# Seven row buffers, x1 parked in DRAM, h2 in one run and a shorter expert search in a fused transformer layer

## What is computed

```
h2 = rms_norm(x1, norm2_g) * (1 + scale2) + shift2
q = (h2 @ w_query).reshape(T, 8, 2, 64)
s = einsum('thpd,hpnd->thpn', q, sub_keys)          # 8 heads, 2 halves, 128 keys
s_top, i_top = top_k(s, 16)
cand = s_top[:, :, 0, :, None] + s_top[:, :, 1, None, :]   # 16 x 16 pairs
best, bi = top_k(cand.reshape(T, 8, 256), 16)
ia, ib = bi // 16, bi % 16
e = i_top[.., 0][ia] * 128 + i_top[.., 1][ib]       # one of 16384 experts
g = softmax(best)
a = gelu(einsum('tkd,td->tk', u_table[e], h2))
y = einsum('tk,tkd->td', g * a, v_table[e])
out = x1 + gate2 * y
```

## Time and profile before

| | |
|---|---|
| median of 3 runs | 1573.08 us (1570.5 to 1574.24) |
| the profiled execution | 1575.63 us, span 1573.1 us |
| PE busy | 1449.0 us (92%) |
| DVE busy | 1265.0 us (80%) |
| ACT busy | 706.4 us (45%) |
| POOL busy | 768.1 us (49%) |
| moved by DMA | 434.68 MB, mean 276 GB/s |
| chain that ended last | PE 66%, DVE 10%, POOL 9%, DMA 8%, ACT 3% |

### The profile page before, as it was taken

How to read it: one execution, slowest core, us unless ns; L and a number is a source line. 1 busy time by engine, 2 the same in 40 slices (tenths; PEclk the granted TensorE clock), 3 DMA queues, 4 the chain that set the end, 5 groups by cost and what they waited for, 6 DMA issues and landing times.

```text
span 1573.1 us, 23445 instructions
## 1 busy us (share of the span) xinstructions
PE 1449.0 (92%) x8439; PEld 1332.0 (85%) x8439; DVE 1265.0 (80%) x2583; ACT 706.4 (45%) x1311; POOL 768.1 (49%) x478
## 2 busy tenths in 40 slices
PE   3898999989999899998999899767999999999998
PEld 3465566867999889998999899767999999999998
DVE  3857676874999678976889785578999999899996
ACT  1235465332434677346763585213334333333431
POOL 2001000111677677776777777883455455354541
PEclk9999579999999999999999999998999999999999
DMA  9720100443667699997899888999999999999994
GB/s 325 276 106 1 54 1 1 160 147 117 223 231 241 225 310 321 382 321 260 306 348 362 286 294 321 383 341 350 367 384 381 390 372 387 371 389 372 378 393 173
DMA packets 157970, 434.68 MB, mean 276 GB/s; under 512 B 16736, under 2 KB 50848, under 8 KB 156960
## 3 DMA queue, kind: packets, MB, share of 16 engines
q1 hardware_dynamic: 91200, 240.36, 43.1%
q0 software_dynamic: 46080, 167.79, 28.3%
q10 hardware_dynamic: 20576, 25.05, 4.4%
HBM read 388.02 MB, written 45.12 MB: 275 GB/s over the span
## 4 chain that ended last, share of the span: by engine, by line
PE 66%; DVE 10%; POOL 9%; DMA 8%; ACT 3%; issue 3%; ACTq 0%; SPq 0%; DVEq 0%
PE ps L1174 10%; PE ps L1175 10%; PE ps L1176 10%; POOL lo L519 6%; DMA rows<-in_u_rows,E 5%; PE ps L1123 5%; PE ps L1125 4%; PE ps L1124 4%; PE ps L893 4%; PE ps L1134 2%; PE ps L1010 2%; POOL rows L531 2%; PE ps L980 2%; PE ps L993 1%; PE ps L983 1%
## 5 line engine op out<-in xcount | busy, mean ns | idle before, releaser
L519 POOL TENSOR_TENSOR lo<-raw,hi 128x1024 fp32r<-128x1024 f32 x128 | 327.9, 2566 | 195.9 <-ACT hi L757 195.3
L757 ACT ACTIVATE hi<-raw 128x1024 fp32r<-128x1024 f32 x256 | 271.0, 1059 | 292.5 <-PE ps L1176 211.8
L1123 PE MATMUL ps<-h2hi,hi 128*128 128x352 f32 x1024 | 346.7, 339 | 25.8 <-POOL lo L519 24.8
L1125 PE MATMUL ps<-h2hi,lo 128*128 128x352 f32 x1024 | 340.1, 332 | 0.0
L1174 PE MATMUL ps<-chi,hi 128*128 128x352 f32 x1000 | 322.6, 323 | 16.9 <-DVE lo L1588 16.9
L1124 PE MATMUL ps<-h2lo,hi 128*128 128x352 f32 x1024 | 337.9, 330 | 0.0
L1175 PE MATMUL ps<-clo,hi 128*128 128x352 f32 x1000 | 322.3, 322 | 0.0
L1176 PE MATMUL ps<-chi,lo 128*128 128x352 f32 x1000 | 322.3, 322 | 0.0
L531 POOL DMA_INDIRECT rows<-in_v_tiles,E x96 | 153.3, 1597 | 151.2 <-DVE y_tok L1601 121.4
L1123 PEld LDWEIGHTS ps<-h2hi,hi 128*128 128x128 f32 x1024 | 196.8, 192 | 30.9 <-POOL lo L519 29.6
L1174 PEld LDWEIGHTS ps<-chi,hi 128*128 128x128 f32 x1000 | 188.5, 188 | 17.2 <-DVE lo L1588 17.2
(11 more groups left out here) (288 smaller groups left out, 2272.2 us busy)
## 6 DMA issues: line engine op xcount, KB each, us to landing
raw<-in_u_tiles SPq DMA_DIRECT2D x128, 512.0 KB, 5.0
raw<-in_v_tiles SPq DMA_DIRECT2D x128, 512.0 KB, 6.6
gelus<-act_out ACTq DMA_DIRECT2D x128, 176.0 KB, 5.2
act_in<-gelus SPq DMA_DIRECT2D x128, 176.0 KB, 7.8
gates<-stage SPq DMA_DIRECT2D x32, 512.0 KB, 7.3
gate<-gates SPq DMA_DIRECT2D x32, 512.0 KB, 7.7
late<-in_w_ada SPq DMA_DIRECT2D x4, 2048.0 KB, 8.6
qkT<-in_w_ada SPq DMA_DIRECT2D x3, 2048.0 KB, 14.1
```

The lines of the kernel that those rows point to most:

```text
L519: nc.gpsimd.tensor_tensor(lo[m % 3][:], raw[m % 3][:], hi[m % 3][:].bitcast(F32), ALU.subtract).then_inc(u_lo, 1)
L757: nc.scalar.activation(hi[m % 3][:], raw[m % 3][:], ACT.Copy).then_inc(t_hi, 1)
L1123: nc.tensor.matmul(out, hi[n % 3][:, cols], dense(h2hi, k), start=(k == 0), stop=False)
L1125: last = nc.tensor.matmul(out, lo[n % 3][:, cols], dense(h2hi, k), start=False, stop=(k == KD - 1))
```

## The change

- Two more row buffers; four of the seven lie where `res` was. x1 is stored to DRAM once it is complete, and loaded back behind the last row sum; the final additions wait for it.
- h2's parts lie as [chunk, token]: one run of 352 per chunk.
- 136 candidates a head instead of 256: the first eight of the first list with all sixteen of the second (128), and the last eight of the first with the best of the second. The index arithmetic puts position 128 + i back to the pair (8 + i, 0).
- The index search is fused: both halves together, sixteen operations (compare and multiply in one) that each write every sixteenth element of a [2, 8, 16, 16] tile, and one reduce.
- Fifteen pauses are placed in a search instead of four, each with one row dot (`FILL` = 15); build steps take two rows each. S0 is 11, SEARCH 17, so the tail has 22 dot steps. EARLY is 4, MORE is 4, `more_at` two steps earlier.
- A gather may go behind a low part one step earlier (m - 2), and the first seven gathers stand behind low part 13.
- On ACT the wait for the stored gates stands ahead of the gate copies instead of ahead of the weighing, and the last three high parts of c ahead of the gelu. On DVE the first weighings and low parts of the second product are reordered.

```diff
-S0, SEARCH, BUILD, GP, GB = 12, 18, P // (2 * HB), 16, 4
-NROWS = 5
+S0, SEARCH, BUILD, GP, GB = 11, 17, P // (2 * HB), 16, 4
+NROWS = 7
+NC = KTOP // 2 * (KTOP + 1)
...
-        (h2hi, h2lo), at3 = region(at2, [("h2hi", [P, T // XT, KD, XT], F32R), ("h2lo", [P, T // XT, KD, XT], F32R)])
+        (h2hi, h2lo), at3 = region(at2, [("h2hi", [P, KD, T], F32R), ("h2lo", [P, KD, T], F32R)])
...
-        (row_hi,), _ = region(at2 + ND * KD * P * 4, [("row_hi", [P, D], F32)])
-        (row_lo,), _ = region(at2 + (TT + ND) * KD * P * 4, [("row_lo", [P, D], F32)])
+        row_res, _ = region(BASE, [(f"row_res{b}", [P, D], F32) for b in range(4)])
...
-        FILL, PER_BUILD, EARLY, MORE = (1, 1, 2, 2), (2, 3), 12, 6
+        FILL, PER_BUILD, EARLY, MORE = 15, 2, 4, 4
...
-            row_step += [search_at[p] + 3 * (j + 1) for j in range(sum(FILL))]
-            row_step += [build_at[p] + i for i in range(steps_of[p]) for _ in range(PER_BUILD[i % 2])]
+            row_step += [search_at[p] + 1 + j for j in range(FILL)]
+            row_step += [build_at[p] + i for i in range(steps_of[p]) for _ in range(PER_BUILD)]
...
-        more_at = tail_at + 3 + (SU - SLOTS) // 3
+        more_at = tail_at + 5 + (SU - SLOTS) // 3
...
+            sp.wait_ge(x1_ready, KD)
+            sp.dma_start(x1, res[:]).then_inc(x1_out, 16)
...
-                    if m == search_at[p - 1] + 12:
+                    if m == search_at[p - 1] + 10:
...
+            sp.wait_ge(row_used, 2 * SU)
+            sp.dma_start(res[:], x1).then_inc(x1_in, 16)
...
-                while g < 2 * SU and (row_step[g - NROWS] <= m - 3 if g >= NROWS else m >= S0 + 2):
+                while g < 2 * SU and (row_step[g - NROWS] <= m - 2 if g >= NROWS else m >= S0 + 2):
...
                 if n in building:
                     p, i = building[n]
+                    for half in range(2):
+                        weigh_one_hot(p, i, half)
+                    gelu(n)
                     if i == 0 and p >= 2:
                         act.wait_ge(g_out, 16 * GP * (p - 1))
                     for half in range(2):
-                        weigh_one_hot(p, i, half)
-                    gelu(n)
-                    for half in range(2):
                         copy_gates(p, i, half)
                     continue
+                if n >= NT - 3:
+                    high_c(n - (NT - 3))
...
-                settled(tt_(cand[:], sv[:, :, 0, :].unsqueeze(3).to_broadcast([P, PH, KTOP, KTOP]),
-                           sv[:, :, 1, :].unsqueeze(2).to_broadcast([P, PH, KTOP, KTOP]), ALU.add))
+                half = KTOP // 2
+                first, second = sv[:, 0, :, :], sv[:, 1, :, :]
+                tt_(cand[:, :, 0:half * KTOP].rearrange("p h (i j) -> p h i j", j=KTOP),
+                    first[:, :, 0:half].unsqueeze(3).to_broadcast([P, PH, half, KTOP]),
+                    second.unsqueeze(2).to_broadcast([P, PH, half, KTOP]), ALU.add)
+                settled(tt_(cand[:, :, half * KTOP:NC], first[:, :, half:KTOP], second[:, :, 0:1].to_broadcast([P, PH, half]), ALU.add))
...
-                for half in range(2):
-                    settled(tt_(eq, abf[:, half, :, :].unsqueeze(3).to_broadcast([P, PH, KTOP, KTOP]),
-                               iota[:, 0:KTOP].unsqueeze(1).unsqueeze(1).to_broadcast([P, PH, KTOP, KTOP]), ALU.is_equal))
-                    settled(tt_(eq, eq, sixf[:, :, half, :].unsqueeze(2).to_broadcast([P, PH, KTOP, KTOP]), ALU.mult))
-                    settled(nc.vector.tensor_reduce(IJW[:, half, :, :], eq, X, ALU.add))
+                settled(nc.vector.scalar_tensor_tensor(out=bia[:, 0, :, :].bitcast(F32), in0=abf[:, 0, :, :], scalar=float(half),
+                                                       in1=abf[:, 1, :, :], op0=ALU.is_ge, op1=ALU.mult))
+                tt_(abf[:, 0, :, :], abf[:, 0, :, :], bia[:, 0, :, :].bitcast(F32), ALU.add)
+                settled(tt_(abf[:, 1, :, :], abf[:, 1, :, :], bia[:, 0, :, :].bitcast(F32), ALU.subtract))
+                for j in range(KTOP):
+                    last = nc.vector.scalar_tensor_tensor(
+                        out=eq[:, :, :, :, j], in0=abf[:], scalar=float(j),
+                        in1=sixf[:, :, :, j].unsqueeze(3).to_broadcast([P, 2, PH, KTOP]),
+                        op0=ALU.is_equal, op1=ALU.mult)
+                    if j % 6 == 5:
+                        pause()
+                settled(last)
+                settled(nc.vector.tensor_reduce(IJW[:, 0:2, :, :], eq[:], X, ALU.add))
+                pause()
...
             for n in range(EARLY):
                 row_sum(n)
-                if n >= EARLY - 3:
-                    weigh(n - (EARLY - 3))
-                    low_c(n - (EARLY - 3))
+            weigh(0)
+            weigh(1)
+            low_c(0)
+            weigh(2)
+            low_c(1)
             low_v(0)
+            low_c(2)
             low_v(1)
...
+            dve.wait_ge(x1_in, 16)
```

More of the change, by code:

```diff
@@ L164, in build @@
         rows, at4 = region(at4, [(f"rows{b}", [P, D], F32) for b in range(3)])
-        (row_hi,), _ = region(at2 + ND * KD * P * 4, [("row_hi", [P, D], F32)])
-        (row_lo,), _ = region(at2 + (TT + ND) * KD * P * 4, [("row_lo", [P, D], F32)])
+        row_res, _ = region(BASE, [(f"row_res{b}", [P, D], F32) for b in range(4)])
         x_part = rows[0]
-        rows = [t[:] for t in rows + [row_hi, row_lo]]
+        rows = [t[:] for t in rows + row_res]
         (late,), at_l = region(END - KD * CH * 4, [("late", [P, KD, CH], F32)])
@@ L1069, in _ @@
             pe.wait_ge(w_hi, 3)
-            product4(("query", 0), lambda k: h2hi[:, :, k, :], lambda k: h2lo[:, :, k, :], h2_hi, h2_split, 3, qp_ps)
+            product4(("query", 0), lambda k: h2hi[:, k, :], lambda k: h2lo[:, k, :], h2_hi, h2_split, 3, qp_ps)
             modulation(10)
@@ L1077, in _ @@
                 pe.wait_ge(qp_sb, h - 3)
-                product(ps[:, h % 4, :], ("query", 1), (h % 4) * P, lambda k: h2hi[:, :, k, :], lambda k: h2lo[:, :, k, :]).then_inc(qp_ps, 1)
+                product(ps[:, h % 4, :], ("query", 1), (h % 4) * P, lambda k: h2hi[:, k, :], lambda k: h2lo[:, k, :]).then_inc(qp_ps, 1)
                 if h == 6:
@@ L1463, in _, with top16, settled_after_pause @@
             dve.sem_inc(ada_read, 1)
-            def top16(vals, idx, lists, n, between, fills):
+            def top16(vals, idx, lists, n, pause):
+                def settled_after_pause(ins):
+                    steps[0] += 1
+                    ins.then_inc(dve_step, 1)
+                    pause()
+                    dve.wait_ge(dve_step, steps[0])
                 for a in range(n):
                     last = nc.vector.max(vals(a)[:, 0:8], lists(a))
-                settled(last)
+                settled_after_pause(last)
                 for a in range(n):
                     last = nc.vector.max_index(idx(a)[:, 0:8], vals(a)[:, 0:8], lists(a))
-                settled(last)
-                between(fills[0])
+                settled_after_pause(last)
                 for a in range(n):
                     last = nc.vector.match_replace(lists(a), vals(a)[:, 0:8], lists(a), -3.0e38)
-                settled(last)
+                settled_after_pause(last)
                 for a in range(n):
                     last = nc.vector.max(vals(a)[:, 8:16], lists(a))
-                settled(last)
-                between(fills[1])
+                settled_after_pause(last)
                 for a in range(n):
                     last = nc.vector.max_index(idx(a)[:, 8:16], vals(a)[:, 8:16], lists(a))
-                settled(last)
+                settled_after_pause(last)
             def row_dot(g):
@@ L1491, in row_dot, with search @@
                                                accum_out=aa[:, g:g + 1]).then_inc(row_used, 1)
-            def search(p, between):
+            def search(p, pause):
                 if p == 0:
@@ L1497, in search @@
                     dve.wait_ge(s_in, p * 16)
-                top16(lambda a: sv[:, a % PH, a // PH, :], lambda a: six[:, a % PH, a // PH, :], lambda a: s[:, a, :], 2 * PH, between, FILL[0:2])
+                top16(lambda a: sv[:, a // PH, a % PH, :], lambda a: six[:, a // PH, a % PH, :], lambda a: s[:, a, :], 2 * PH, pause)
                 dve.sem_inc(s_free, 1)
@@ L1532, in one_hot @@
                     .then_inc(oh_ready, 1)
-            tt_(x_part[:].rearrange("p (k g c) -> p g k c", k=KD, c=XT), gathered(h2hi).bitcast(F32), gathered(h2lo).bitcast(F32), ALU.add)\
+            tt_(x_part[:].rearrange("p (k c) -> p k c", k=KD), gathered(h2hi).bitcast(F32), gathered(h2lo).bitcast(F32), ALU.add)\
                 .then_inc(x_cols, 1)
-            settled(search(0, lambda count: None))
+            settled(search(0, lambda: None))
             def expert_numbers():
@@ L1554, in _ @@
             for p in range(1, TT):
-                search(p, fill).then_inc(ijw_ready, 1)
+                search(p, lambda: fill(1)).then_inc(ijw_ready, 1)
```

45 lines of the change are left out of this document (26 added, 19 removed).

## The result

1527.45 us, the median of four runs (1520.74 to 1529.59), against 1571.79 for the kernel before on the same chip (four runs, 1569.83 to 1574.24): a ratio of 0.971, 95% interval 0.9676 to 0.9744. Forecast 1524. The profiled execution took 1529.59 us, its span is 1527.8. In each table and sum here gelu(n) is, as ahead, where dot step n has ended. Only on the way into the second product is that not so in every kernel: ScalarE can stand waiting for DVE there while its gelu is due, and the end of the dots is then read from PE.

What follows compares the result with a forecast made beforehand. It took TensorE to bound searches and second product, late rows the builds, POOL the tail. Stretches summed: 443.8 to gelu(12), first search to 523, builds and searches to 919.6, tail to 1024.1, second product 498.5: 1524 us, range 1504 to 1556.

Steps and rivals of the forecast that it cites:

- builds: Build stretches: seven buffers, two rows a step and the earlier gate end the wait for rows; 5.65 us a step.
- second product: Second matmul product: 502.1 us falls to 498.5; eight more row sums come in, DMA needs 390 GB/s.
- rival (1): DMA ceiling of 363 GB/s binds in searches 2 and 3 and the second product: 1559 us; chance 0.10.
- h2: Query and dot matmuls: one run saves 9.4 and 5.7 ns a matmul; +18 us in all if nothing.
- rival (3): h2's layout gives nothing because the 5.7 ns belongs to the bank order: 1542 us; chance 0.07.
- tail: Last dot steps, from gelu(106) to the end of dot 127: low parts 6.0 us apart, 104.5 us.
- The search itself: Searches on DVE: shorter candidate lists, index search 10.7 us plus 7 us more of waits a search.
- Row dots: Searches: rows go from 6 to 15 at 1.22 us, +11 us of DVE; DVE sets the pace at 71 us.
- First gathers: Start of the first search: seven leave together, 2.4 us more between low parts 13 and 14; index wait goes.
- (2): Short index-search operations each wait about 2 us for POOL, +26 us a search: 1594 us, slower; chance 0.05.
- (4): Rows still late in the builds, 6.1 to 6.4 us a step: 1544 to 1557 us; chance 0.13.
- (5): No DMA ceiling at all, searches at 67 us: 1506 us; chance 0.15.

Runs made afterwards that it cites:

- e4: The changed kernel with h2's parts laid out as before, in 11 runs of 32 per chunk: 1533.43 us, ratio 0.9748.
- e9: The kernel of e8 with h2's parts in 11 runs of 32 again: 1508.17 us, ratio 0.9571.
- e5: The changed kernel with the index tile's sixteen positions outermost, so products write without gaps and the reduce reads 1 KB apart: 1527.42 us, ratio 0.9706.
- e11: The changed kernel with only the first seven gathers spread, two behind each low part from low part 14 on: 1528.2 us, ratio 0.9705.
- e8: The kernel of e7 with the first seven gathers spread, two behind each low part from low part 14 on: 1497.19 us, ratio 0.9512.
- e1: The kernel before with only the gather gate moved one step earlier (m - 2 for m - 3): 1532.96 us, ratio 0.9747.
- e2: The changed kernel with the gather gate taken back to m - 3: 1533.78 us, ratio 0.9753.
- e3: The changed kernel with five row buffers instead of seven: 1532.9 us, ratio 0.9742.
- e7: The changed kernel with six row dots a search instead of fifteen, two or three in turn per build step: 1502.77 us, ratio 0.9541.
- e10: The changed kernel with every second store of the gates made twice, to another DRAM tensor: 1542.15 us, ratio 0.9796.

## Why the prediction was right, and where not

**Right, and borne out.** The *builds*: 90.4 said, 90.2 measured, no wait on rows. The *second product*: 386 to 395 GB/s in eight windows of 50 us from 1050 on, with PE at 316 matmuls or more in each. ScalarE does wait for raw tiles there, which I had named as a sign against me, but 14 times and never over 2.0 us, and PE has no gap from it. So rival (1) falls, and so does the sum of some 1568 us that I worked out by the 358 GB/s of the Trainium skill (DMA: Bandwidth & Descriptors, "Specifications"). The page works that figure out as the stack's 716 GB/s divided by two cores, and this kernel runs on one. So the figure did not apply here, and no run says anything about it with both cores at work. *h2*: the query line takes 7.25 us where it took 7.57, a dot 3.84 against 3.82 said, so rival (3) falls; e4 and e9 give 6 and 11 us against the 18 of its full sum. The *candidates*: MAX8 over 136 takes 1.71 us for eight, 1.7 said. *x1*: the reload is issued at 1508.1 and lands at 1515.8, so DVE waits 6.0 us for it, where I had it start some 7 us ahead of the first slice; that costs nothing, because DVE then does four slices in 2.73 us and waits for PE from the fifth on, as read from the earlier trace rows. The *tail* is 2.5 us shorter than the model (104.5 said, 102.0 from gelu(106) to gelu(127)), not traced further, and the gap is nothing: the first matmul on chi starts 0.15 us after the last of the dots, at full clock, where the kernel before waited 16.89 us and started at the lower one.

```profile
471.61 1.71 DVE L1483 MAX8 best<-cand 128x8 f32<-128x136 f32 x8
...
1029.55 0.32 PE L1134 MATMUL ps<-h2hi,lo 128*128 128x352 f32 x1
1029.70 0.32 PE L1183 MATMUL ps<-chi,hi 128*128 128x352 f32 x1
...
1515.81 2.73 DVE L1664 SCALAR_TENSOR_TENSOR res<-ps,ada,res 128x512 f32<-128x512 f32 x4 [6.01 <-DMA res<-x]
1518.93 0.75 DVE L1664 SCALAR_TENSOR_TENSOR res<-ps,ada,res 128x512 f32<-128x512 f32 x1 [0.40 <-PE ps L1204]
```

**Wrong (1): the waits in "The search itself".** I had written that the forecast is wrong if the search stretch passes 80 us. Search 1 took 85.4, against 79.2 summed, and search 2 took 79.8 where 70 to 76 were to be seen. I took 5.4 us for the sixteen products and 7 us for waits, with 1 more in "Row dots". In search 1 the products take 15.8 us, and three other short operations 7.6 (3.10 on line 1529, 2.33 on line 1533 and 2.14 on line 1552, at 519.94); unheld they take 0.2 to 0.3 each. Line 1529 is held in this search alone, the other two in all three (1.7 to 2.3 and 2.1 to 2.2). In search 2 the sixteen take 19.6, in search 3 13.4. Two terms were mis-sized: the bare price, 0.49 instead of 0.34 from start to start (I read it off a contiguous write, and e5 shows that this is the difference), and the holds. The seven microseconds I took were near the 7.9 by which search 1's products were held (11.7 in search 2, 5.5 in search 3). What I left out is that the two short operations ahead of them and the one behind them are held like them, and I did not see that single-input operations on unsigned integers and casts (2.43 us for one at 636.98 in the new kernel, 0.30 at 470.01) can be held as well. The trace of the kernel before had it: the same cast took 2.12 us at 471.16.

**Wrong (2): "First gathers ... the wait for the indices goes".** I counted 2.4 us for two more gathers and let the wait vanish. The indices of search 0 were ready at 443.9, so the first gather waited 3.85 us, and seven gathers together kept low part 14 until 455.1: step 14 took 15.3 us instead of 3.84. In search 1 that wait did not decide (e11), because DVE was later still. In e8, with a lighter DVE, it is worth 5.6 us. Search 1 as a whole ended 5 us later than said, at 528.1.

**Right by its own working, but the sum hid the cause: "Builds".** The text credits seven buffers, two rows a step and the gate together, with arrival 13 us and wanted time 22. Its own numbers for the kernel before say that the gate alone is enough: 18 - 5.7 = 12.3 us is before 14. The lower rate and the buffers together are enough without the gate: wanted at 22, after 18. And with the gate the buffers add nothing there: five of them at two rows are wanted at 2.5 x 5.7 + 2.4 = 16.7, after 13. e1, e2 and e3 show these three. The lower rate alone would not be enough by the same numbers, 16.7 against 18, and the buffers alone just so (2.8 x 5.7 + 2.4 = 18.4 against 18); neither was run. A slack term is a threshold, not a price to be shared out, and I should have costed each part alone.

**Not weighed enough: "Row dots".** I saw that nine more rows cost 11 us of DVE a search, that DVE would set the pace there, and that it had room in the builds. That this makes the part a loss of its own was not drawn. e7 gives 25 us for taking it back.

**The rivals.** (2), held short operations, was the right mechanism at a third of its size: the sixteen are held 7.9 us in search 1 against 26 there. (4) fell with the builds, (5) with the searches. The searches of e8, at 67.6, 67.9 and 67.3, have the length that (5) gave, but by another way: it takes rows out of them, and does not lift a limit of the DMA. The time came out 3.5 us above the forecast because 10 us more in the searches met 5 us less elsewhere; that closeness is partly luck.

## What to carry to other kernels

For a gather in an in-order queue work out two times, when the row arrives and when it is wanted, for each part of a change by itself: once the first is earlier, more buffers or a lower rate buy nothing more for that wait. Here one step in the gate was 39 of 44 us. Before work is put into the pauses of another engine's stretch, ask which engine ends that stretch: nine row dots of 1.22 us in each search cost 25 us where the builds had room for them for nothing. And many short operations on DVE are each a new chance to wait for one of POOL's low parts, so a fused form that is shorter on paper may come out even.

## What the hardware showed that I had not expected

- Operations of DVE with a single unsigned input were held as well: the 128-element one of line 1529 took 3.10 us (0.22 for its twin), and ended at 490.44, just behind a low part that had begun after it; the cast at 636.98 took 2.43 and ended at 639.41, as the low part from 636.85 to 639.26 did. POOL in the first case:

```profile
486.94 0.96 POOL L540 DMA_INDIRECT rows<-in_u_rows,E  x1
487.92 2.42 POOL L527 TENSOR_TENSOR lo<-raw,hi 128x1024 fp32r<-128x1024 f32 x1
```

  That the shared port of which the prediction speaks is the cause was not tried by itself.
- The other direction too: in the kernel before, the issue of an indirect DMA took POOL 3.07 us instead of 0.95, beside a DVE product of 2048 elements with two inputs.

```profile
506.65 2.29 DVE L1515 TENSOR_TENSOR cand<-abf,iota 128x2048 f32<-128x2048 f32 x1
...
506.71 3.07 POOL L531 DMA_INDIRECT row_hi<-in_u_rows,E  x1 [0.15 <-issue]
```

- A gap costs DVE in either direction: 622 against 414 ns for 256 elements written 64 bytes apart, 7.5 against 4.4 us for 4096 elements read 1 KB apart (e5).
- One core moved 395 GB/s over 50 us with PE at full pace, and 415 over the 80.9 us of the second search in e10.
